# RMS factors behind the product: both gated feed-forwards and the linear attention multiply the raw residual

## The reference

```python
for i in range(2):
    hn = rms_norm(h, attn_norm[i])
    mix = dilated_attention_mixer(hn, ...) if i == 0 else gla_mixer(hn, ...)
    h = h + mix
    h = h + swiglu(rms_norm(h, ffn_norm[i]), ffn_w_gate_up[i], ffn_w_down[i])

def rms_norm(x, gain):
    return x * lax.rsqrt(jnp.mean(x * x, axis=-1, keepdims=True) + 1e-6) * gain
def swiglu(h, w_gate_up, w_down):
    g, u = jnp.split(h @ w_gate_up, 2, axis=-1)
    return (jax.nn.silu(g) * u) @ w_down
```

## Time and profile before

| what | value |
|---|---|
| median of 3 runs | 1674.65 us (1667.18 to 1675.72) |
| span of the profiled execution | 1673.7 us |
| PE busy | 1607.3 us, 96% |
| DVE busy | 1133.9 us, 68% |
| ACT busy | 817.7 us, 49% |
| weights high half (L190), x198 | 372.7 us on ACT |
| weights low half (L206), x200 | 459.6 us on DVE |

### The profile page before, as it was taken

The page is one execution under the profiler, slowest core; times in us unless marked ns, Lnnn a source line. Parts: engine busy times, 40 slices in busy tenths (PEclk is TensorE's granted clock), DMA queues, the critical chain, the costliest instruction groups (busy, mean ns, idle before and its releaser), DMA issues. The chain is left out here.

```text
span 1673.7 us, 24996 instructions
## 1 busy us (share of the span) xinstructions
PE 1607.3 (96%) x10054; PEld 1410.0 (84%) x10054; DVE 1133.9 (68%) x1539; ACT 817.7 (49%) x1057; POOL 298.7 (18%) x239
## 2 busy tenths in 40 slices
PE   8999999999999998999999999989899999999997
PEld 7878889799987886899888788669698888889986
DVE  6777766588876575677467564368887565667864
ACT  5436555544434563544444454465444554355643
POOL 4644340000000010000005200047465000000000
PEclk9999999999999999999999999989999999999999
DMA  7554331387794441786454222000000265555643
GB/s 264 190 175 151 125 128 51 101 269 253 232 328 168 151 151 51 259 294 203 155 194 133 76 80 76 0 20 1 1 1 4 84 210 181 179 161 180 192 174 114
DMA packets 155394, 240.96 MB, mean 144 GB/s; under 512 B 12272, under 2 KB 80624, under 8 KB 155152
## 3 DMA queue, kind: packets, MB, share of 16 engines
q1 hardware_dynamic: 141632, 208.69, 38.0%
q0 software_dynamic: 6816, 27.08, 4.4%
q10 hardware_dynamic: 6832, 3.59, 0.8%
HBM read 238.29 MB, written 1.05 MB: 143 GB/s over the span
## 5 line engine op out<-in xcount | busy, mean ns | idle before, releaser
L206 DVE TENSOR_TENSOR wlo<-raw,whi 128x2048 fp32r<-128x2048 f32 x200 | 459.6, 2311 | 161.2 <-ACT whi L190 160.1
L190 ACT ACTIVATE whi<-raw 128x2048 fp32r<-128x2048 f32 x198 | 372.7, 1887 | 245.6 <-PE ps L340 161.6
L338 PE MATMUL ps<-xf,whi 128*128 128x256 f32 x1056 | 296.1, 280 | 2.9 <-DVE xf L488 1.0
L339 PE MATMUL ps<-xf,whi 128*128 128x256 f32 x1056 | 295.2, 280 | 0.0
L340 PE MATMUL ps<-xf,wlo 128*128 128x256 f32 x1056 | 295.2, 280 | 0.0
L338 PE MATMUL ps<-whi,xs 128*128 128x512 f32 x672 | 267.5, 398 | 5.7 <-DVE xs L481 3.5
L340 PE MATMUL ps<-whi,xs 128*128 128x512 f32 x672 | 262.6, 391 | 0.0
L339 PE MATMUL ps<-wlo,xs 128*128 128x512 f32 x672 | 261.9, 390 | 0.0
L338 PEld LDWEIGHTS ps<-xf,whi 128*128 128x128 f32 x1056 | 198.8, 188 | 5.5 <-issue 5.4
L339 PEld LDWEIGHTS ps<-xf,whi 128*128 128x128 f32 x1056 | 200.3, 190 | 0.0
L340 PEld LDWEIGHTS ps<-xf,wlo 128*128 128x128 f32 x1056 | 198.8, 188 | 0.0
(11 more groups left out here) (377 smaller groups left out, 2685.7 us busy)
## 6 DMA issues: line engine op xcount, KB each, us to landing
raw<-in_ffn_w_gate_up SPq DMA_DIRECT2D x88, 512.0 KB, 4.9
raw<-in_a_w_in SPq DMA_DIRECT2D x72, 512.0 KB, 4.5
raw<-in_w_in SPq DMA_DIRECT2D x60, 512.0 KB, 4.4
wide<-in_w_mod POOLq DMA_DIRECT2D x24, 1024.0 KB, 7.2
raw<-in_w_up SPq DMA_DIRECT2D x44, 512.0 KB, 4.6
raw<-in_ffn_w_down SPq DMA_DIRECT2D x40, 512.0 KB, 4.5
raw<-in_b_w_in SPq DMA_DIRECT2D x24, 512.0 KB, 4.5
raw<-in_w_down SPq DMA_DIRECT2D x20, 512.0 KB, 4.3
```

Of the source, the lines that this page charges most:

```text
L190: self.hi_ok.inc(act.activation(self.whi[:, h % NHI, 0:nk, :], self.raw[:, h % NRAW, 0:nk, :], ACT.Copy))
L206: self.lo_ok.inc(dve.tensor_tensor(self.wlo[:, h % NRAW, 0:nk, :], self.raw[:, h % NRAW, 0:nk, :], self.whi[:, h % NHI, 0:nk, :].bitcast(F ...
L338: pe.matmul(o, ahi, bhi, start=start, stop=False)
L339: pe.matmul(o, ahi, blo, start=False, stop=False)
```

## The change

- **Three handovers** use `Deferred` in place of `Norm`. The transposes read `resid` itself, in parts: columns 0 to 511 of both tiles between the last product's tile 0 and tile 1 (`early_pe`), columns 512 to 1023 of tile 0 behind tile 1 (`tile_0_pe`), those of tile 1 inside the next product, behind its first quarter half (`tile_1_pe`). The split applies the gain alone. There are no `keep_warm` matmuls.
- **The factor** is computed beside: both tiles' squares, one root, one reciprocal. `rows_pe` spreads it over the partitions (two matmuls of 128 columns), `rows_dve` copies it from PSUM.
- **Feed-forwards A and B**: a new DVE operation per chunk multiplies the gate half by the row of factors before silu; the value half keeps raw, and the factor of its token is applied as the down product is added to the residual.
- **Layer B**: the gate input is multiplied by the row; q and k keep raw; v takes the square of the factor and r the factor, as ACT's scale, by tile (two ACT operations of 512 columns in place of one of 1024); the head's norm takes the factor too, one small DVE operation more per head. The gate product stands behind the first half of q.
- **Modulation**: chunk 7 moves from feed-forward A to B: 22 passes over 15 slots with shares 4 (up) and 5 (down), and 10 over 8 slots.
- The weights' rings are unchanged; ACT and DVE split the next chunk's first halves (`nxt[1]`, `nxt[2]`) inside the handover. Some buffers move.

```diff
+    class Deferred:
+        def early_pe(self):
+            pe.wait_ge(added.sem, self.at + 1)
+            for g in range(2):
+                self.group_pe(g, (0, 1))
+        def tile_0_pe(self):
+            pe.wait_ge(xs_lo.sem, self.hi0 + 2)
+            pe.wait_ge(added.sem, self.at + 2)
+            for g in range(2, 4):
+                self.group_pe(g, (0,))
+            xs_want[:] = [self.hi0 + 2, self.hi0 + 4]
+        def tile_1_pe(self):
+            pe.wait_ge(added.sem, self.at + 3)
+            for g in range(2, 4):
+                self.group_pe(g, (1,))
+        def rows_pe(self):
+            pe.wait_ge(st_ready.sem, self.ready)
+            for t in range(TT):
+                i_ = pe.matmul(ps[:, 6, t * P:(t + 1) * P], self.r[:, t:t + 1].to_broadcast([P, P]), ident, start=True, stop=True)
+            tile_ok.inc(i_)
+        def on_act(self, nxt):
+            self.parts.on_act((0, 1))
+            W.hi(nxt[1])
+            self.parts.on_act((2, 3))
+            W.hi(nxt[2])
+            for t in range(TT):
+                act.wait_ge(added.sem, self.at + t + 2)
+                as_.inc(act.activation(self.sq, resid[:, t, :], ACT.Square, scale=D ** -0.5, accum_out=self.r[:, t:t + 1]))
+                act.wait_ge(as_.sem, as_.n)
+            st_rt.inc(act.activation(self.r, self.r, ACT.Sqrt, bias=eps_col))
+        def on_dve(self, nxt):
+            W.lo(nxt[1])
+            self.parts.on_dve((2, 3))
+            W.lo(nxt[2])
+            dve.wait_ge(st_rt.sem, self.root)
+            st_ready.inc(dve.reciprocal(self.r, self.r))
...
@@ ffn, on PE, on ACT and on DVE
-                chunk_pairs(up[ci], 2 * (ci % 2), xf)
+                chunk_pairs(up[ci], 2 * (ci % 2), x, {(0, 0): pre.tile_1_pe, (1, 1): pre.rows_pe} if pre is not None and ci == 0 else None)
...
+                if pre is not None:
+                    act.wait_ge(ff_y.sem, y0 + ci + 1)
+                    ff_act.inc(act.activation(tmp[:, par, :, :], tmp[:, par, :, :], ACT.Silu))
...
+                if pre is not None:
+                    W.wait_used(dve, up[ci][1])
+                    if ci == 0:
+                        pre.rows_dve()
+                    if ci >= 2:
+                        dve.wait_ge(ff_val.sem, v0 + ci - 1)
+                    ff_y.inc(dve.tensor_tensor(tmp[:, par, :, :], blocks[:, 0:2], bc(pre.rb, 1, 2), ALU.mult))
...
+                    added.inc(dve.scalar_tensor_tensor(o, pv, pre.r[:, t:t + 1], o, ALU.mult, ALU.add))
...
@@ layer_b, on PE
             at_.meet(pe)
-            gw.product()
-            chunk_feat(chunks[0], range(0, 4))
+            pe.wait_ge(md_out.sem, MOD_A)
+            chunk_feat(chunks[0], range(0, 4), seq=1, between={(0, 0): pre.tile_1_pe, (0, 3): gw.product, (1, 1): pre.rows_pe})
...
@@ layer_b, on ACT and DVE
-                lb_evac.inc(act.activation(o_, ps[:, (4 + 2 * j) % 8:(4 + 2 * j) % 8 + 2, :], ACT.Copy if j < 2 else ACT.Silu))
+                for t in range(TT):
+                    i_ = act.activation(o_[:, t], ps[:, (4 + 2 * j) % 8 + t, :], ACT.Copy if j < 2 else ACT.Silu,
+                                        scale=(r_sq if j < 2 else pre.r)[:, t:t + 1])
...
+            vs.inc(dve.tensor_tensor(st[:, h], st[:, h], pre.r, ALU.mult))
...
-    mod = Modulation(range(8), 15, Carve(start=6152)(2, CW), Carve(start=11264)(2, CW))
+    mod = Modulation(range(MOD_A), [4] * N_FFC + [5] * 4, Carve(start=6152)(2, CW), Carve(start=5120)(2, CW))
...
-    mod = Modulation(range(8, 12), 8, Carve(start=3072)(2, CW), None)
+    mod = Modulation(range(MOD_A, 12), [1] * 8, Carve(start=3072)(2, CW), None)
```

More of the change, by code:

```diff
@@ L368, in chunk_tok, with chunk_feat @@
                 W.used.inc(i_)
-    def chunk_feat(chunk, banks, both=False, blocks=range(4), keep=False, stage=None):
+    def chunk_feat(chunk, banks, both=False, blocks=range(4), keep=False, stage=None, seq=0, between=None):
         n = 2 * SEQ if both else SEQ
@@ L384, in chunk_feat, with chunk_pairs @@
                     else:
-                        rh, rl = xs[:, 0, kk, :], xs[:, 1, kk, :]
+                        rh, rl = xs[:, 2 * seq, kk, :], xs[:, 2 * seq + 1, kk, :]
                     i_ = mm3(ps[:, b, 0:n], wh[:, k, mb * P:(mb + 1) * P],
                              wl[:, k, mb * P:(mb + 1) * P], rh, rl, s == 0 and k == 0, s == 1 and k == HK - 1)
-            if not keep:
+                if mb == 3 and not keep:
+                    W.used.inc(i_)
+                if between is not None and (s, mb) in between:
+                    between[s, mb]()
+            if blocks[-1] != 3 and not keep:
                 W.used.inc(i_)
         return i_
-    def chunk_pairs(chunk, bank, x):
+    def chunk_pairs(chunk, bank, x, between=None):
         for s, half in enumerate(chunk):
@@ L403, in chunk_pairs @@
                              s == 0 and k == 0 and mb % 2 == 0, s == 1 and k == HK - 1 and mb % 2 == 1)
-            W.used.inc(i_)
+                if mb == 3:
+                    W.used.inc(i_)
+                if between is not None and (s, mb) in between:
+                    between[s, mb]()
     class Split:
@@ L544, in build, with last_tok @@
     added = Signal(nc, "dve", "tile_added")
-    def last_tok(chunk, banks, seq):
+    def last_tok(chunk, banks, seq, behind=None):
         for t, b in enumerate(banks):
@@ L559, in last_tok @@
                 tile_ok.inc(i_)
+            if behind is not None:
+                behind[t]()
     def wait_tile(eng, t, half):
@@ L651, in on_dve @@
             o = resid[:, :, 0:CW]
+            if deferred:
+                added.inc(dve.tensor_tensor(o, o, ps[:, b0:b0 + 2, :], ALU.add))
+                W.lo(nxt[0])
+                for t in range(TT):
+                    o = resid[:, t, CW:D]
+                    wait_tile(dve, t, chunks[1][1])
+                    added.inc(dve.tensor_tensor(o, o, ps[:, b1 + t, :], ALU.add))
+                    if t == 0:
+                        norm.parts.on_dve((0, 1))
+                norm.on_dve(nxt)
+                return
             if gate is None:
@@ L709, in build, with ffn @@
     DOWN = ((0, (HK, HK)), (8, (HK, HK)), (16, (HK, 2)))
-    def ffn(up, down, nxt, norm, conv=None, gate=None, beside=None, at_=None, ahead=None, mod=None):
+    def ffn(up, down, nxt, norm, conv=None, gate=None, beside=None, at_=None, ahead=None, mod=None, x=xf, pre=None):
         c = Carve(end=HID)
@@ L854, in on_dve @@
                 W.wait_used(dve, down[0][2][1])
+                if pre is not None:
+                    for t in range(TT):
+                        i_ = dve.scalar_tensor_tensor(o[:, t], pv[:, t], pre.r[:, t:t + 1], o[:, t], ALU.mult, ALU.add)
+                    (added if deferred else vs).inc(i_)
+                    continue
                 if gate is not None:
@@ L873, in ffn @@
         on_dve()
-        norm.split(*nxt[1:], **({} if ahead is None else {"ahead": ahead}))
+        if not deferred:
+            norm.split(*nxt[1:], **({} if ahead is None else {"ahead": ahead}))
     md_sil = Signal(nc, "act", "mod_silu", False)
@@ L1061, in layer_a @@
         tabs = c(2, NG, 2, TT, A_HD)
-        r1, r2 = c(16), c(16)
         X = c(1024)
@@ L1394, in layer_a @@
         on_pool()
-        norm.split(nxt[1])
     lb_w = Signal(nc, "dma", "b_gate_weights")
@@ L1471, in project_pe @@
             pe.wait_ge(lb_evac.sem, 1)
-            chunk_feat(chunks[1], range(0, 4))
+            chunk_feat(chunks[1], range(0, 4), seq=1)
             pe.wait_ge(lb_t1.sem, 1)
```

145 lines of the change are left out of this document (105 added, 40 removed).

## The result

The changed kernel is slower by 0.75%: 1683.97 us median of eight runs (1682.22 to 1690.64) against 1671.24 for eight runs of the kernel before, a ratio of 1.0075 (95% interval 1.0055 to 1.0095). Forecast was 1667.5, that is some 7 us faster than the 1674.65 of the first three runs of before; measured is 12.7 us slower than the eight.

The account below looks back on a forecast made before the run. PE was taken to bound almost everything, so gains lay only at the three handovers. Feed-forward A -1.4, layer B +7.0, heads -0.3 and feed-forward B +2.0 sum to 7.3 us faster: 1667.5 us, range 1660 to 1674.

Parts of the forecast that it names:

- The three handovers: PE's gap from the last product's end to the next stage's matmul is four transposes, 0.45 us, at all three places.
- the sum: Into layer B: 0.9+0.9+0.3 and 120 matmuls (14.1) are 16.2 us against 23.2, gain 7.0.
- T+16.9: Into feed-forward A: T is the end of the last product's tile 1; DVE's copied factor row ends 16.9 us later.
- the waits in the up product: Feed-forward A: PE waits 6.3 us in all for low weight halves, 5.5 more than before.
- Layer B's 7.0: The handover into layer B gains 7.0 us and keeps it, as all engines behind its start shift together.
- The heads: Layer B: one DVE operation of about 0.2 us per head, on PE's path once, at the last head: 0.3.
- the wait before the spreading matmuls: Handover into feed-forward A: PE waits 0.8 to 0.9 us for the factor, whose reciprocal is done at T+10.2.
- DVE ends its eleventh chunk some 2.7 later, which costs PE about 0.6 before the second down chunk.: Feed-forward A, up product into down product: DVE's lateness of 2.7 us makes PE wait about 0.6.
- DVE has room: Feed-forward B: the factor is there early; PE waits 1.8 us before chunk 2 and hardly again.
- the third handover: Layer B into feed-forward B: 4.7 us less 1.8 of waits and 0.9 for the moved modulation chunk, gain 2.0.
- The third: the clock: Rival: the granted clock falls once at every handover, 5 us go, 1672.5; chance 0.15 together with handovers keeping their length.
- the slower one: Rival: DVE bounds both feed-forwards if the multiply with its round trip costs over 1.8 us; about 1682; chance 0.1.

Follow-up runs that it names:

- e9: Kernel before with only the handover into layer B deferred, no multiply, modulation as before: 1663.88 us, 0.9959 of before.
- e8: Changed kernel with no handover deferred and no multiply, keeping the new modulation deal and moved buffers: 1686.96 us, 1.0091 of before.
- e5: Changed kernel with the modulation's sums over partitions one slot earlier on PE in feed-forward A alone: 1675.5 us, 1.0032 of before.
- e1: Changed kernel with the modulation's sums over partitions one slot earlier on PE in both feed-forwards: 1681.18 us, 1.0059 of before.
- e6: As e5, with feed-forward B's modulation passes dealt anew (1,1,2,1,1,2,1,1): 1675.09 us, 1.0029 of before.
- e13: As e4, with feed-forward B's modulation loads waiting only for the last add, not the reciprocal: 1662.51 us, 0.9939 of before.
- e14: As e6, with fewer modulation passes beside A's first chunks and both feed-forwards' modulation loads waiting only for the last add: 1662.93 us, 0.9946 of before.
- e2: Changed kernel without the multiply of the gate half by the factors in feed-forwards A and B: 1680.84 us, 1.0059 of before.
- e4: Changed kernel with only the handovers into layer B and feed-forward B deferred, no multiply in A, modulation as before: 1663.79 us, 0.9956 of before.
- e3: Changed kernel with the modulation dealt as in the kernel before: 1673.14 us, 1.0008 of before.
- e10: As e4, with feed-forward B's modulation passes dealt later, none beside its first chunk: 1665.75 us, 0.9962 of before.
- e11: Changed kernel with unread filling matmuls where PE waited for low weight halves, too many of them: 1724.38 us, 1.0296 of before.
- e12: As e11, with fewer filling matmuls (4, 3 and 7 in place of 14, 13 and 28): 1683.05 us, 1.0056 of before.

## Why the prediction was wrong, by its own steps

**Right.** The three handovers: 0.36 us between the products where 0.45 was said, and 15.6 us behind the product in layer B for the 15.3 that the sum has without the early transposes, whose 0.9 came as said. DVE's row in A: the multiply at T+16.9 was put at 345.6 and stands at 345.56 (T of before plus 0.9 for the early transposes); the round trip is 1.39 for 1.35; the waits in the up product are 6.6 for 6.3. That product ends 0.6 later than before; my terms make it 0.8. Layer B's 7.0 is 7.5, and alone, in e9, 0.41% of the median or 6.9 us. The heads cost about 0.2 for 0.3. Of the signs that were named in advance, the gaps, the round trip and A's waits came; the wait before the spreading matmuls was 0.2 for 0.9, since the reciprocal stood at T+9.5 and not at T+10.2, and DVE's busy time in A stayed under 105 us.

**The step that failed first: "DVE ends its eleventh chunk some 2.7 later, which costs PE about 0.6 before the second down chunk."** The wait there was 3.3 us and not 0.6, a second one of 6.6 before the fifth down chunk stood in no term, and with the clock the down product lost 15.5 us. I followed DVE's list and the weights through eleven chunks and stopped there. I had counted the moved chunk as 0.9 us less PE work and the shares as a number of passes per chunk. I put the new order of the sums at nothing without a reason, and never asked which wait ties a pass to PE: the sums' wait stands in the class that the diff touches. e8 shows both waits without any handover (10.2 us in that product), e5 and e1 take them away with one slot. DVE's lateness had nothing to do with them.

**The second: "DVE has room", in feed-forward B, a wait of 1.8.** It was 4.2 by the waits, and with a fall of the clock behind it (1.7) and the moved chunk's 0.9 B's up product took 8.7 us more (the rest, some 2, is the transposes and spreading matmuls inside it and the pace of the last section); the third handover with it, forecast at a gain of 2.0, lost about 3.2 (8.7 less the 5.5 by which B starts sooner). DVE's passes were one part (e6: the wait fell from 3.5 to 1.9 us), the late loads another (e13, e14). I had listed what the changed step issues on PE, ACT and DVE and left out POOL's loads, whose start hangs on the handover's last operation.

**The third: the clock.** I set it against the handovers, where it did not fall: in none of the three is there a half-clock stretch. It fell behind the four long waits inside the feed-forwards, so the waits that I did forecast were also priced too low, by half of 3.4 us: the 3.6 us before chunk 2 cost some 5.3. In all, clock 0.986 against 0.992 over the span is 10 us, and these 10 lie inside the losses above and are not added to them. Of the 20 us between forecast and measurement about 15 belong to the first step and 5 to the second.

**Of the rivals** the slower one (DVE bounds both feed-forwards, chance 0.1) had the sign but not the mechanism: its point was a round trip over 1.8 us, and it is 1.39; a chunk with one pass takes DVE under PE's 11.3, and e2, without the multiply, is still 0.59% slower than before. That the kernel was near the 1682 of this rival is chance. That the new deal of the modulation loses by itself was no rival of mine, though it is the largest single term.

**What the change is worth.** Its handover into layer B gains 0.4% alone. That the one into feed-forward B is worth anything is not shown: without the earlier loads e4 is level with e9, and with them e13's B ends its up product 4.5 us before e9's, but 2.8 of these arose ahead of layer B, and the intervals of the two ratios overlap. The one into feed-forward A starts it 5.5 us sooner and spends them. The best of the runs, e13, is 0.61% faster than before (interval 0.49 to 0.73).

## What to carry to other kernels

When a change deals side work anew, follow each wait of that work both ways, not only its busy time: an engine may wait for a result that the other gives only behind its own wait, and such a ring cost the same here whether the engine came late to it or not. When a stage is made to start sooner, ask of every transfer of that stage what releases it; one that still waits for the old event now collides with what it used to precede. And price a wait of several microseconds on PE with the clock that may fall behind it.

## What the runs showed of the hardware

The pace of 256-column matmuls is at one of two levels, with the granted clock at 1.00 in both. The last feed-forward's up product has the same code in all kernels and keeps one level throughout; before, then after (windows):

```profile
1479.20:1603.60 124.40, 124.40 (x1056) 124.40 (x1057) 96.98 (x125) 73.23 (x83) 0.00 (x0) 1.00 0.58 183
```
```profile
1491.20:1610.90 119.70, 119.70 (x1056) 119.70 (x1057) 96.85 (x125) 73.46 (x83) 0.00 (x0) 1.00 0.61 190
```

That is 118 ns for one against 113, 4.7 us for the stage. In feed-forwards A and B the level changes from chunk to chunk: before has 118 in A's first four chunks and 113 to 114 in the next four. The Trainium skill, "TensorE: Matmul & The Clock Gate", section "Back-to-back issue gap", gives for one matmul apart from others the columns over 2.4 GHz and 2.5 ns more, which is 109 ns here, and says that in a stream the weight loads share in setting the spacing; no chunk of these up products got to 109, and the measurement decides. Of the profiled executions those of before, e3, e8, e10 and e11 had the slow level there and the other eleven the fast one; no edit goes with it. So two single executions are compared stage by stage, and medians decide.

The half-clock stretches also differ where the code does not. In layer C there were 13.6 us of them in before, after and seven more executions, 20.4 in e6 and e14, and 27.2 in e4, e5, e8, e11 and e13. B's down product and layer C together took 671.3 to 671.8 us with 13.6 (670.4 in e12), 673.4 and 673.7 with 20.4, and 676.0 to 676.4 with 27.2. What brings them there no run shows.
